# Two chained blocks in fp32: weight products of the second part as plain fp32 matmuls instead of products of split halves, and all 32 hidden tiles of each MLP kept

## The reference

```python
def second_block(x, meta_tokens, ...):
    h = concatenate([meta, x], axis=1)               # 528 tokens
    for layer in range(2):
        u = rmsnorm(h, attn_norm_g[layer])
        if layer % 2 == 0:
            mix = ab_mixer(u, w_in_ab, ...)          # projection 1024 -> 2832, gated delta rule both ways,
                                                     # banded attention, then @ w_out_ab (1024 x 1024)
        else:
            mix = c_mixer(u, w_qkv_c, ...)           # projection 1024 -> 1536, rotary attention, @ w_out_c
        h = h + mix
        u = rmsnorm(h, mlp_norm_g[layer])
        h = h + square(relu(u @ w_ff1[layer])) @ w_ff2[layer]    # 1024 -> 4096 -> 1024
    return h[:, 16:]
```

## Time and profile before

| | us |
|---|---|
| median of 3 runs | 3808.87 |
| their range | 3789.22 to 3822.9 |
| the profiled execution | 3807.15 |
| its span | 3805.4 |
| mean granted TensorE clock | 0.85 of full |
| busy: PE / DVE / ACT / POOL | 2685.4 / 2037.5 / 802.3 / 1864.6 |

### The profile page before, as it was taken

How to read it: one execution, slowest core, us unless ns; L and a number is a source line. 1 busy time by engine, 2 the same in 40 slices (tenths; PEclk the granted TensorE clock), 3 DMA queues, 4 the chain that set the end, 5 groups by cost and what they waited for, 6 DMA issues and landing times.

```text
span 3805.4 us, 40545 instructions
## 1 busy us (share of the span) xinstructions
PE 2685.4 (71%) x15872; PEld 2087.4 (55%) x15872; DVE 2037.5 (54%) x4133; ACT 802.3 (21%) x1515; POOL 1864.6 (49%) x1389
## 2 busy tenths in 40 slices
PE   6521887207852287543767888888899998999999
PEld 4410444103431144211225777777789997789999
DVE  6589877888787878588444534454220103532010
ACT  2100111001110011111113322332332322433231
POOL 0166655775567756477752322221354543126463
PEclk7665998558986599766998988898899999999999
DMA  5398889997999879999981200000123332012332
GB/s 172 128 309 301 279 286 334 321 340 259 313 322 333 310 267 345 332 339 341 356 306 34 67 23 1 1 1 1 56 73 95 89 87 59 23 45 78 95 94 78
DMA packets 417984, 694.02 MB, mean 182 GB/s; under 512 B 35784, under 2 KB 280691, under 8 KB 417667
## 3 DMA queue, kind: packets, MB, share of 16 engines
q0 software_dynamic: 147456, 536.94, 39.7%
q1 hardware_dynamic: 270339, 154.50, 13.9%
HBM read 689.26 MB, written 2.10 MB: 182 GB/s over the span
## 4 chain that ended last, share of the span: by engine, by line
PE 51%; DVE 16%; POOL 13%; DMA 10%; issue 6%; ACT 3%; SPq 1%; DVEq 0%; ACTq 0%
PE PS L1593 25%; POOL ring L601 13%; DMA ring<-in_peer_v,eidx 7%; PE PS L768 6%; DMA ring<-in_peer_u,eidx 2%; PE PS L747 2%; DVE ring L1301 2%; PE PS L1495 1%; PE PS L1504 1%; PE PS L653 1%; PE PS L1501 1%; DVE X L1316 1%; PE PS L1603 1%; DVE W L1175 1%; PE PS L1615 1%
## 5 line engine op out<-in xcount | busy, mean ns | idle before, releaser
L601 POOL DMA_INDIRECT ring<-in_peer_u,eidx x512 | 635.8, 1242 | 404.0 <-DVE eidx L1278 177.9
L601 POOL DMA_INDIRECT ring<-in_peer_v,eidx x512 | 588.0, 1148 | 351.4 <-PE PS L768 192.1
L1593 PE MATMUL PS<-held_uH,GW 128*128 128x264 f32 (+1 forms) x3648 | 693.1, 290 | 35.9 <-POOL BIG_value L2120 31.8
L1301 DVE CUSTOM_DVE_ANT_0 ring<-ring,hn 128x1024 f32<-128x1024 f32 x512 | 614.7, 1223 | 115.6 <-DMA ring<-in_peer_u,eidx 106.8
L2106 POOL TENSOR_TENSOR GW<-held_wr,GW 128x1024 fp32r<-128x1024 f32 x178 | 428.6, 2409 | 453.2 <-ACT GW L1883 453.2
L768 PE MATMUL PS<-ring,dg 128*128 128x512 f32 x1024 | 528.2, 655 | 172.4 <-DMA ring<-in_peer_v,eidx 168.0
L1593 PEld LDWEIGHTS PS<-held_uH,GW 128*128 128x128 f32 x3648 | 581.7, 193 | 48.9 <-issue 32.4
L1593 PE MATMUL PS<-BIG_value,GW 128*128 128x264 f32 (+1 forms) x1824 | 486.1, 287 | 0.0
L768 PEld LDWEIGHTS PS<-ring,dg 128*128 128x128 f32 x1024 | 196.2, 206 | 460.6 <-DMA ring<-in_peer_v,eidx 276.6
L1316 DVE SCALAR_TENSOR_TENSOR X<-ring,gact,X 128x1024 f32<-128x1024 f32 x256 | 328.6, 1284 | 186.0 <-DMA ring<-in_peer_v,eidx 181.4
L1593 PE MATMUL PS<-hid,GW 128*128 128x264 f32 (+1 forms) x3072 | 370.4, 282 | 0.0
(11 more groups left out here) (465 smaller groups left out, 3613.2 us busy)
## 6 DMA issues: line engine op xcount, KB each, us to landing
held_wr<-in_w_ff SPq DMA_DIRECT2D x128, 512.0 KB, 4.0
wqr<-in_peer_wq SPq DMA_DIRECT2D x64, 512.0 KB
held_wr<-in_w_in_ab SPq DMA_DIRECT2D x18, 512.0 KB, 3.9
ring<-in_peer_u,eidx POOLq DMA_INDIRECT x512
ring<-in_peer_v,eidx POOLq DMA_INDIRECT x512
BIG<-in_w_in SPq DMA_DIRECT2D x4, 1536.0 KB, 11.4
held_wr<-in_w_qkv_c SPq DMA_DIRECT2D x12, 512.0 KB, 3.8
w_out<-in_w_out SPq DMA_DIRECT2D x1, 4096.0 KB, 19.0
```

The lines of the kernel that those rows point to most:

```text
L601: e.indirect_dma_start(out=ring[:, i % RING, :], out_offset=None, in_=rows_u if k < HK else rows_v, in_offset=bass.IndirectOffsetOnAxis(ap ...
L1301: e.tensor_tensor_reduce(row, row, hn[:, :], 1.0, 0.0, ALU.mult, ALU.add, act[:, k:k + 1]).then_inc(*n.up(e_dot))
L1593: ins = e.matmul(bank[b + a][:, 0:w], w_[:, k * P:(k + 1) * P], x_[:, c0:c0 + w], start=(first and z in (0, 2)), stop=(last and z >= 4))
```

## The change

All weight products of the second part become plain fp32 matmuls: for each chunk and each half of the tokens one instruction, taking the weight from the DMA ring `wr` and the operand from `uT` or `hid` directly. `high`, `low`, `high_half`, `low_half` go, and so do the rings and tiles that held halves; a slot of `wr` is free when the unit's products are done (`g_done`). The delta rule's scratch of direction 0 and the banded attention's lay over the halves' memory and get their own. In the MLP `hid` holds all 32 tiles (as much memory as 16 high and 16 low ones), so it runs 32 units of the first layer and then 8 output tiles with 4 units each; each output tile is added to `hT` once, where it was added twice. The weights are loaded in that order.

```diff
     def load_weight(e, i):
         slot, src = i % NW, weights[i]
         if i >= NW:
-            e.wait_ge(w_lo, i - NW + 1)
+            e.wait_ge(g_done, i - NW + 1)
...
             for q, src in enumerate(operands):
                 i = count["unit"]
                 count["unit"] += 1
-                e.wait_ge(w_lo, i + 1)
-                hi, lo = r(wH[i % NS]), r(wL[i % NS])
+                e.wait_ge(d_f[i % NW], loaded[i])
                 for k in range(8):
-                    x_hi, x_lo, ready = src[k]
+                    x_, ready = src[k]
                     if ready:
                         e.wait_ge(*ready)
-                    first, last = q == 0 and k == 0, q == len(operands) - 1 and k == 7
-                    for z, (w_, x_, a) in enumerate(((hi, x_hi, 0), (hi, x_lo, 0), (hi, x_hi, 1), (hi, x_lo, 1),
-                                                     (lo, x_hi, 0), (lo, x_hi, 1))):
-                        c0, w = sp.halves[a]
-                        ins = e.matmul(bank[b + a][:, 0:w], w_[:, k * P:(k + 1) * P], x_[:, c0:c0 + w],
-                                       start=(first and z in (0, 2)), stop=(last and z >= 4))
+                    for a, (c0, w) in enumerate(sp.halves):
+                        ins = e.matmul(bank[b + a][:, 0:w], wr[:, i % NW, k, :], x_[:, c0:c0 + w],
+                                       start=(q == 0 and k == 0), stop=(q == len(operands) - 1 and k == 7))
                 ins.then_inc(*up(g_done))
...
         def norm(from_k, sp=ALL):
             for k in range(from_k, 8):
                 sums(ones2, sq[k % 2], k == 0, k == 7, sp)
-            return normed()
+            return [(uT[:, k, :], nxt(n_u)) for k in range(8)]
...
         def mlp(last):
             sp = LATE if last else ALL
             ops = norm(7, sp)
-            for half in range(2):
-                for m in range(16):
-                    gemm([ops], m_val, sp)
-                    ops = waited(ops)
-                hops = [(r(hid[:, 0, m, :]), r(hid[:, 1, m, :]), nxt(lo_g)) for m in range(16)]
-                residual([hops[0:8], hops[8:16]], half and not last, sp)
+            hops = []
+            for m in range(32):
+                b = gemm([ops], m_val, sp)
+                ops = waited(ops)
+                hops.append((hid[:, m, :], freed[b]))
+            residual([hops[8 * q:8 * q + 8] for q in range(4)], not last, sp)
...
     def second_scalar(e, n):
...
-        def high(i):
-
-            e.wait_ge(d_f[i % NW], loaded[i])
-            if i >= NS:
-                e.wait_ge(g_done, i - NS + 1)
-            e.copy(r(wH[i % NS]), wr[:, i % NW].rearrange("p k n -> p (k n)")).then_inc(*up(w_hi))
...
         def norm(sp=ALL):
-            d = sp.cut(R)
-            sqrt(e, n, d)
-            for k in range(8):
-                e.wait_ge(*nxt(n_u))
-                high_half(sp.cut(uH[:, k, :]), sp.cut(uT[:, k, :]))
+            sqrt(e, n, sp.cut(R))
...
         def mlp(l, last):
             sp = LATE if last else ALL
             norm(16 + 8 * l, sp)
-            for half in range(2):
-                for m in range(16):
-                    b = output()
-                    e.wait_ge(*nxt(m_relu))
-                    if m >= 2:
-                        e.wait_ge(lo_g, lows[0] + m - 1)
-                    e.tensor_tensor(sp.two(value[:, m % 2, :]), sp.two(sq[m % 2]), sp.pair(b), ALU.mult).then_inc(*up(m_val))
-                    count["hi"] += 1
-                lows[0] += 16
-                residual(2, sp)
+            for m in range(32):
+                b = output()
+                e.wait_ge(*nxt(m_relu))
+                e.tensor_tensor(sp.two(hid[:, m, :]), sp.two(sq[m % 2]), sp.pair(b), ALU.mult).then_inc(*up(m_val))
+            residual(4, sp)
```

## The result

| | us |
|---|---|
| kernel before, median of 4 runs beside it | 3814.86 (3789.22 to 3822.9) |
| kernel after, median of 4 runs | **3979.36** (3975.07 to 3986.41) |
| ratio | **1.0445**, 95% interval 1.0391 to 1.05 |
| profiled execution of after, and its span | 3986.41, 3984.5 |
| mean granted TensorE clock | 0.863 |

The forecast was 3982 us, range 3952 to 4015, slower: it came true. The plain products cost what the rows of the kernel before said. That the median lies within 3 us of the forecast is partly luck: four runs of the kernel before alone spread over 34 us, and the change between the medians is 164.5 us where +173.5 was forecast.

What follows compares the result with a forecast made beforehand. TensorE's products were taken to bound 128 of 178 units, the halves costing nothing there. Terms 102.5 + 88.0 - 12 - 3 - 2 = +173.5 us on the profiled 3807.15 gave 3980.7, predicted as 3982 us, range 3952 to 4015.

Steps and rivals of the forecast that it cites:

- The price of a unit: Weight products: a plain unit of 32 records takes 7.11 us (528 tokens) or 6.90 (512), against 5.86 and 5.66.
- two-records-of-two-cycles reading: Plain matmuls already in the kernel: each instruction is two records, each two cycles per column plus 2.3 ns.
- each record carries some 12 ns on top: Split products before: each of a unit's 48 records costs one cycle per column plus some 12 ns, which go.
- The three norms: Norms ahead of both MLPs and the projection, with the unit behind each: -3.9 us each, -12 in all.
- Ahead of the delta rule: 22 units: 14 cost +17.5 us, convolution gives -2, waits and half clock -14.3; with an earlier start, together -3.
- the convolution units: Eight units ahead of the delta rule, 8.26 us apart, become 8.0 apart, set by TensorE: -2 us.
- `w_out_ab`: Eight TensorE-bound units behind the heads' sum, each +1.25 us: +10.
- The last attention: Eight casts leave ScalarE, whose copies TensorE awaits 6.4 us in all: -2 us (0 to -6).
- The MLP's order and the loads: Fewer adds on an idle VectorE, and loads landing in 4.0 us with 21 us to spare: 0 and 0.
- The delta rule's stretch: Delta rule and banded attention keep the same instructions: 0; a move by more than a few us would be something missed.
- What waits give back: 178 longer units would cost 222 us; waits return about 49.
- The rivals: Surcharge per pass: 4103 us, chance 0.03; lower clock: 4081, 0.03; one record per instruction: about 3370, 0.02; 90 us returned: near 3930, 0.02.

Runs made afterwards that it cites:

- experiment 1: Kernel before with every weight product one plain fp32 product of the high halves, all halves still made and waited for: 4002.56 us, ratio 1.0535.
- experiment 2: Kernel before with the last 72 units' split products 512 columns wide instead of two of 256: 3804.54 us, ratio 1.0001.
- experiments 2 and 4: The second mixes forms in the kernel before: plain ahead of the delta rule and first behind norms, split elsewhere, late 512 columns, casts behind the root: 3785.38 us, 0.994.
- experiment 5: Kernel after with the MLP's work and loads in the old order, two halves of sixteen tiles: 3967.05 us, ratio 1.0429.
- experiment 6: Kernels before and after, both unchanged, executed once more under the profiler: 3794.98 and 3973.19 us.
- experiment 7: Mixed-form kernel with only twelve convolution units plain ahead of the delta rule: 3790.3 us; a second kernel also casting three weights ahead of the root: 3786.08 us.

## Why the prediction was right, and where it was not

**The price of a unit** is right: 7.12 and 6.91 us for 7.11 and 6.90, from line 653's instruction and the `sums`, and experiment 1 shows it alone. The two-records-of-two-cycles reading held at 256, 264 and 512 columns. By the passes alone that the Trainium skill counts (FP8 and Floating Point Precision, TensorE Precision Notes) a unit would have gone up by 4/3; the measured ratio is 7.12 / 5.86 = 1.215. The trace agrees with four passes for a plain product, but not with the count as a price, since a pass of the split form costs more than one cycle per column.

**Why the split form costs more** was read wrongly. The prediction had "each record carries some 12 ns on top" and "the 48 surcharges of 12 ns go". The 12 ns are right as a difference at this shape, and so the unit's price is; as a price per record they fell in experiment 2. No term of the sum rested on it, but the -18 us expected of experiments 2 and 4 did, and gave 4.

**The three norms**: -3.9 each forecast. Ahead of the first MLP it was -4.4, with TensorE's start 5.83 us behind the sum's reading (5.6 forecast) and a unit of 9.14 (9.6); ahead of the projection -4.7, ahead of the second MLP -3.4 (below). Together -12.5 for -12: right.

**Ahead of the delta rule**: -3.0 for -3, but the parts were not all right, and that their errors cancel is luck. Cut once more at the start of the thirteenth unit (2151.79 in before, 2151.74 in experiment 1, 2159.62 in after), it is 123.6, 124.2 and 114.5 us from the first norm's sum, then 87.1, 93.2 and 93.2 us to the delta rule. So dropping the halves gives 9.7 us, all ahead of the thirteenth unit; the forecast's terms for that (4.05, 2.5, 2.2 and 2) make 10.8. The longer units cost 0.5 us ahead of it, since they fill the waits of 4.7 and 8.1 us named in experiment 1, and 6.1 behind it. A term was missing there, and it is the step that failed: two of the last four units of the kernel before pay for half clock, and plain ones don't. TensorE's chain before, the thirteenth unit and these two, then the latter in experiment 1:

```profile
2151.79 8.12 PE PS L1593 x48
...
2211.33 7.44 PE PS L1593 x48
...
2222.35 8.61 PE PS L1593 x48
```

```profile
2218.02 7.32 PE PS L1591 x32
...
2228.43 7.32 PE PS L1591 x32
```

A unit of this stretch is 6.04 us at full clock. The granted clock was 0.79 and 0.67 in the two of before, and 1.00 from 2200 to 2243 us in experiment 1, whose gaps there are as long. That is 4.0 us, and 0.5 in the `spread`s between; the forecast had it at nothing. The 3 us of half clock behind the wait of 4.73 it did have, and they were 3.1 (2.12 for 1.08 in the `spread`, 8.12 for 6.04 in the unit).

Against that the convolution units gave nothing. They were forecast 8.0 apart; ScalarE's copies (timeline of after) are 8.30 apart, for 8.26 before, though VectorE's first instruction has fallen to 0.49 as said:

```profile
2084.93 0.60 ACT L1890 COPY raw<-PS 128x528 f32<-128x528 f32 x1 [2.79 <-PE PS L1570]
...
2093.23 0.60 ACT L1890 COPY raw<-PS 128x528 f32<-128x528 f32 x1 [2.61 <-PE PS L1570]
```

ScalarE waits for TensorE, so TensorE does set the distance, as forecast, but its chain has 7.32 us for such a unit and 0.99 for the `sums` behind it, where the forecast had 7.11 and 0.89. The -2 for these units was 0. Why a unit is 0.2 us longer here than in the MLPs (7.12) was not followed.

**`w_out_ab`**: +8.5 for +10. Not costed: dropping the three casts that ScalarE made ahead of the root. VectorE's reciprocal waited 2.97 us for the root before and waits 0.71 now (timeline of before, then of after):

```profile
2684.99 3.44 DVE L2303 RECIPROCAL BIG<-BIG 4x528 f32<-4x528 f32 x1 [2.97 <-ACT BIG L841]
```

```profile
2688.67 3.44 DVE L2165 RECIPROCAL BIG<-BIG 4x528 f32<-4x528 f32 x1 [0.71 <-ACT BIG L822]
```

That is -2.3, and the root lies on the path. About half of it is lost again: the first two units behind take 17.25 us in after and 16.12 in experiment 1, at granted clocks of 0.84 and 0.90, so from experiment 1 to after the stretch goes from 85.6 to 84.4. The prediction put the stretch of the delta rule at 0 and didn't look at the seam behind it.

**The last attention**: "-2 (0 to -6)" was nearer to -4. TensorE's wait for ScalarE's copies, 6.4 us in the earlier trace rows, is in the kernel after (total us, times, longest):

```profile
PE PS L1747 <- ACT PTc L1974: 2.1, 3, 1.2
```

From the attention's first product to the first unit of `w_out_c` it is 92.2 us in both executions for 95.8 and 96.1, -3.7; experiment 1, which keeps the casts, has 95.7. The rest of that row of the table: the norm ahead gave 4.7 (14.7 us for 19.4) where 3.9 was forecast, and the projection's units +12.5 for +13.75.

**The MLP's order and the loads**: 0 and 0, shown by experiment 5 and by the empty idle column of the page's groups. The second MLP is 2.3 us longer than its term: 63 units at 1.25 instead of 1.24 are 0.6 of it, and the norm there gave 3.4 instead of 3.9 (its sum read to its first eviction, 15.5 us for 18.9). The remaining 1 us is in the units of before: from that eviction (3440.61) to the end of the last product (3795.73) are 63 units of 5.64 us on average, not 5.66.

**The delta rule's stretch** moved by -8 in the first pair, which the prediction said "would be something I missed". It was how the granted clock fell in one execution, as experiment 6 shows. The test was badly chosen: the stretch varies by 11 us between executions of one kernel.

**What waits give back.** The forecast had 49 us, the 222 us of 178 units less the sum. Experiment 1 parts them: 26 us come from dropping the halves, and nearly as much was never paid, since with all halves still made the 178 longer units cost 196 us (6.7 + 189.6) and not 222.

**The rivals.** A surcharge per pass (7.8 us a unit), a clock under full in the MLPs, one record per instruction, and 90 us given back are all refuted by the first three views of the kernel after.

## What to carry to other kernels

Price a replacement from an instruction of its kind that already runs in the kernel, as the time from its start to the next line's start, and multiply by what the bounding engine issues; here that gave 7.11 and 6.90 us a unit for 7.12 and 6.91. Cut both traces at the same events and take two executions of each: the stretches that repeat to 0.1 to 0.6 us carry the change, and one that moves by 11 us by itself carries nothing. A longer product on the bounding engine fills waits beside it, and here it kept two units out of half clock, so it cost less than its length. An operation moved off one wait on the path can land on the next: the casts moved behind the root brought GpSimd's low halves beside VectorE's work, and 2.3 us won became 1.4 to 2.0 lost.

## What was not expected of the hardware

The fp32r products cost more per column than one cycle at 2.4 GHz (0.4167 ns): from 0.1179 us at 256 columns and 0.2325 at 512, a record is 0.4477 ns a column and 3 ns. The line gives 0.1215 at 264 columns, where 0.1221 is measured. The plain ones cost two cycles a column and 2 to 3 ns at 256, 264 and 512 columns. So a weight product in split halves costs 3.27 to 3.33 cycles per column (3 x 0.2325 / 512 and 3 x 0.1221 / 264, over 0.4167 ns) and a plain one 4.05 (6.91 / 16 / 256), nearly whatever the number of records. Why an fp32r column costs more than a cycle, no run here shows.

VectorE can be slowed by GpSimd working beside it: four instructions of the same form took 2.80 us alone and 6.83 beside GpSimd's low halves (experiment 7), and one of 0.50 us took 2.22 while such a low half ran.
